# A two-layer decoder trunk on one core: new start addresses for the weight tiles and the transposed activations of the gate and up products, and four orders of their k steps

## The reference, cut to what matters

```python
def swiglu(x, w_gate, w_up, w_down):
    return (jax.nn.silu(x @ w_gate) * (x @ w_up)) @ w_down

for l in range(DEPTH):                       # DEPTH = 2
    x = x + 0.5 * swiglu(rms_norm(x, ffn1_norm[l]), ffn1_w_gate[l], ffn1_w_up[l], ffn1_w_down[l])
    h = rms_norm(x, mix_norm[l])
    proj = h @ w_in[l]                       # (256, 1024) @ (1024, 1184 + 2048)
    ...
    merged = jax.nn.sigmoid(g_a) * (o_a @ w_branch_a[l]) + jax.nn.sigmoid(g_b) * (o_b @ w_branch_b[l])
    x = x + merged @ w_out[l]
    x = x + 0.5 * swiglu(rms_norm(x, ffn2_norm[l]), ffn2_w_gate[l], ffn2_w_up[l], ffn2_w_down[l])
```

## Time and profile before

| what | value |
|---|---|
| median of 2 runs | 1039.3 us (1039.26 to 1039.33) |
| the profiled execution, its own time | 1040.34 us |
| its span, first to last instruction | 1038.5 us |
| granted TensorE clock | 1.000 |
| TensorE matmul busy (PE) | 1032.4 us, 99% |
| VectorE busy | 718.3 us, 69% |
| ScalarE busy | 586.1 us, 56% |

### The profile page before, as it was taken

The page is one execution under the profiler, slowest core; times in us unless marked ns, Lnnn a source line. Parts: engine busy times, 40 slices in busy tenths (PEclk is TensorE's granted clock), DMA queues, the critical chain, the costliest instruction groups (busy, mean ns, idle before and its releaser), DMA issues.

```text
span 1038.5 us, 15559 instructions
## 1 busy us (share of the span) xinstructions
PE 1032.4 (99%) x5648; PEld 891.7 (86%) x5648; DVE 718.3 (69%) x1132; ACT 586.1 (56%) x935; POOL 61.8 (6%) x71
## 2 busy tenths in 40 slices
PE   8999999999999999999999999999999999999998
PEld 7888888998888888888888888889988888888887
DVE  6766666668786876666687666666688868666665
ACT  6555454466963754554565455455678646454552
POOL 0052000121100000000000000001211000000000
PEclk9999999999999999999999999999999999999999
DMA  7665544455435455655445555534454346545541
GB/s 264 248 225 192 204 162 167 140 183 193 146 123 203 173 187 189 205 189 209 179 147 202 202 192 182 210 136 152 154 203 163 122 163 219 205 163 202 191 173 61
DMA packets 35269, 187.53 MB, mean 181 GB/s; under 512 B 4368, under 2 KB 4384, under 8 KB 20128
## 3 DMA queue, kind: packets, MB, share of 16 engines
q1 hardware_dynamic: 34992, 186.51, 51.0%
q0 software_dynamic: 240, 0.53, 0.2%
HBM read 185.98 MB, written 1.05 MB: 180 GB/s over the span
## 4 chain that ended last, share of the span: by engine, by line
PE 99%; DMA 1%; SPq 0%; DVE 0%; ACT 0%; issue 0%
PE ps L1369 96%; PE ps L1803 1%; PE ps L1393 1%; DMA w_raw<-in_w_ffn 1%; PE ps L1832 1%; PE ps L1868 0%; PE ps L1712 0%; PE ps L1704 0%; PE ps L1414 0%; DVE x_cols L999 0%; ACT w_hi L554 0%; SPq L318 0%; SPq L317 0%
## 5 line engine op out<-in xcount | busy, mean ns | idle before, releaser
L1369 PE MATMUL ps<-hT,w_hi 128*128 128x512 f32 x1408 | 341.3, 391 | 1.9 <-ACT w_hi L554 1.9
L1369 PEld LDWEIGHTS ps<-hT,w_hi 128*128 128x128 f32 x1408 | 258.9, 188 | 52.4 <-ACT w_hi L554 2.1
L884 DVE TENSOR_TENSOR w_lo<-w_raw,w_hi 128x2048 fp32r<-128x2048 f32 x82 | 188.0, 2293 | 87.7 <-ACT w_hi L549 87.7
L1369 PEld LDWEIGHTS ps<-hT,w_lo 128*128 128x128 f32 x1408 | 176.8, 188 | 7.5
L1369 PE MATMUL ps<-hT,w_lo 128*128 128x256 f32 x1408 | 178.3, 279 | 0.0
L1369 PE MATMUL ps<-w_hi,hT 128*128 128x512 f32 (+2 forms) x576 | 174.3, 377 | 0.0
L549 ACT ACTIVATE w_hi<-w_raw 128x2048 fp32r<-128x2048 f32 x85 | 162.0, 1906 | 13.9 <-PE ps L1369 13.2
L1369 PE MATMUL ps<-w_lo,aTh 128*128 128x512 f32 x352 | 137.2, 390 | 0.0
L1369 PE MATMUL ps<-w_hi,aTl 128*128 128x512 f32 x352 | 137.0, 389 | 0.0
L1369 PE MATMUL ps<-w_hi,aTh 128*128 128x512 f32 x352 | 136.8, 390 | 0.0
L578 ACT ACTIVATE S<-ps 128x256 f32<-128x256 f32 x88 | 33.7, 383 | 154.6 <-PE ps L1369 154.6
(11 more groups left out here) (168 smaller groups left out, 952.9 us busy)
## 6 DMA issues: line engine op xcount, KB each, us to landing
w_raw<-in_w_ffn SPq DMA_DIRECT2D x85, 1024.0 KB, 4.9
w_raw<-in_w_ffn SPq DMA_DIRECT2D x90, 512.0 KB, 5.7
w_raw<-in_w_gate SPq DMA_DIRECT2D x16, 1024.0 KB, 5.1
w_raw<-in_w_proj SPq DMA_DIRECT2D x16, 592.0 KB, 4.4
w_raw<-in_w_branch SPq DMA_DIRECT2D x8, 1024.0 KB, 4.8
w_raw<-in_w_out SPq DMA_DIRECT2D x8, 1024.0 KB, 4.8
w_raw<-in_w_uq SPq DMA_DIRECT2D x4, 384.0 KB, 3.0
w_raw<-in_w_ffn SPq DMA_DIRECT2D x4, 256.0 KB, 6.6
```

Of the source, the lines that this page charges most:

```text
L884: dve.tensor_tensor(wl_gu[b], raw_gu[b], wh_gu[b].bitcast(F32), ALU.subtract).then_inc(lo_gu.sem, 1)
L1369: return pe.matmul(dst, w, m, start=start, stop=stop, skip_group_check=True)
```

## The change

The four parts of the diff, in words:

- `hT` gets 12 unused columns behind each block of 512: blocks are `HT_STEP` = 524 columns = 2096 bytes apart (48 modulo 64).
- The gate and up chunks in `w_hi` and `w_lo` get 12 unused columns each: they are `K_STEP` = 140 columns = 560 bytes apart (48 modulo 64). Gate and up half tiles start at their own offsets in each slot, `HI_AT` and `LO_AT` (columns, for b = 0 and 1, gate and up). The low offset is always 8 columns (32 bytes) below the high one.
- In `gate_up` and `gate_up_low_first` the eight k steps run in one of four orders, by b and s (`K_ORDER`). All other functions keep the order 0 to 7.
- ScalarE's and VectorE's splitting instructions write (and VectorE reads back) the tile as 8 or 16 runs of 128 columns with the gaps between, instead of one run. Their number, sizes and order stay. The DMAs, and every wait and signal, stay.

```diff
-LO_SHIFT = 120
-LO_SLOT = GU_COLS + 128
+K_STEP, HT_STEP = P + 12, 2 * SEQ + 12
+HALF_STEP = 9 * P
+PART_SLOT = 2 * HALF_STEP + 64
+HI_AT, LO_AT = ((52, 40), (12, 16)), ((44, 32), (4, 8))
+K_ORDER = (((0, 1, 2, 3, 4, 5, 6, 7), (0, 2, 4, 6, 1, 3, 5, 7)),
+           ((7, 6, 5, 4, 3, 2, 1, 0), (0, 4, 1, 5, 2, 6, 3, 7)))
...
-        w_hi = sb("w_hi", [P, MIX_SLOTS * GU_COLS], F32R)
-        w_lo = sb("w_lo", [P, MIX_SLOTS * LO_SLOT], F32R)
+        w_hi = sb("w_hi", [P, 2 * PART_SLOT + GU_COLS], F32R)
+        w_lo = sb("w_lo", [P, 2 * PART_SLOT + GU_COLS], F32R)
...
+        def chunks(w, i, gate_at, up_at):
+
+            a, step = i * PART_SLOT + gate_at, HALF_STEP + up_at - gate_at
+            return w[:, a:a + 2 * step].rearrange("p (s n) -> p s n", s=2)[:, :, 0:KC * K_STEP]\
+                .rearrange("p s (k n) -> p s k n", k=KC)[:, :, :, 0:P]
+
+        def cols_of(w, c, n):
+
+            k = c // P % KC
+            part = w[:, c // (KC * P), k:k + n // P, :]
+            return part[:, 0, :] if n == P else part
...
+        wh_gu, wl_gu = ([chunks(w, i, *at) for i, at in enumerate(places)] for w, places in ((w_hi, HI_AT), (w_lo, LO_AT)))
...
-        hT = sb("hT", [P, KC, 2, SEQ], F32R)
+        hT_rows = sb("hT", [P, KC * HT_STEP + 32], F32R)
+        hT = hT_rows[:, 0:KC * HT_STEP].rearrange("p (k n) -> p k n", k=KC)[:, :, 0:2 * SEQ].rearrange("p k (s n) -> p k s n", s=2)
...
-                    act.activation(wh_gu[b], raw_gu[b], ACT.Copy).then_inc(hi_gu.sem, 1)
+                    act.activation(wh_gu[b], raw_gu[b].rearrange("p (s k n) -> p s k n", s=2, k=KC), ACT.Copy).then_inc(hi_gu.sem, 1)
...
-                    dve.tensor_tensor(wl_gu[b], raw_gu[b], wh_gu[b].bitcast(F32), ALU.subtract).then_inc(lo_gu.sem, 1)
+                    dve.tensor_tensor(wl_gu[b], raw_gu[b].rearrange("p (s k n) -> p s k n", s=2, k=KC), wh_gu[b].bitcast(F32), ALU.subtract).then_inc(lo_gu.sem, 1)
...
-                        for k in range(KC):
+                        for i, k in enumerate(K_ORDER[b][s]):
                             c = (s * KC + k) * P
-                            high(2 * b + s, wh_gu[b][:, c:c + P], k, k == 0)
+                            high(2 * b + s, cols_of(wh_gu[b], c, P), k, i == 0)
```

More of the change, by code:

```diff
@@ L117, in build @@
-        wl_d = [w_lo[:, 2 * LO_SLOT + i * DN_COLS:2 * LO_SLOT + (i + 1) * DN_COLS] for i in range(2)]
-        mix_raw, mix_hi = ([w[:, i * GU_COLS:(i + 1) * GU_COLS] for i in range(MIX_SLOTS)] for w in (w_raw, w_hi))
-        mix_lo = [w_lo[:, i * LO_SLOT:i * LO_SLOT + GU_COLS] for i in range(MIX_SLOTS)]
-        hT = sb("hT", [P, KC, 2, SEQ], F32R)
+        w_hi = sb("w_hi", [P, 2 * PART_SLOT + GU_COLS], F32R)
+        w_lo = sb("w_lo", [P, 2 * PART_SLOT + GU_COLS], F32R)
+        raw_gu = [w_raw[:, i * GU_COLS:(i + 1) * GU_COLS] for i in range(2)]
@@ new lines, in build @@
+        wh_gu, wl_gu = ([chunks(w, i, *at) for i, at in enumerate(places)] for w, places in ((w_hi, HI_AT), (w_lo, LO_AT)))
+        raw_d = [w_raw[:, 2 * GU_COLS + i * DN_COLS:2 * GU_COLS + (i + 1) * DN_COLS] for i in range(2)]
+        wh_d, wl_d = ([w[:, 2 * PART_SLOT + i * DN_COLS:2 * PART_SLOT + (i + 1) * DN_COLS] for i in range(2)]
+                      for w in (w_hi, w_lo))
+        mix_raw = [w_raw[:, i * GU_COLS:(i + 1) * GU_COLS] for i in range(MIX_SLOTS)]
+        mix_hi, mix_lo = ([w[:, i * PART_SLOT:i * PART_SLOT + GU_COLS] for i in range(MIX_SLOTS)] for w in (w_hi, w_lo))
@@ L561, in third_high @@
                     act.wait_ge(gu_used.sem, gu_used.at(0, 0))
-                    act.activation(wh_gu[0][:, part], third_raw[:, part], ACT.Copy)\
+                    act.activation(cols_of(wh_gu[0], part.start, KC * P), by_chunk(third_raw[:, part]), ACT.Copy)\
                        .then_inc((third_hi, hi_gu)[half].sem, 1)
@@ L715, in _ @@
                         act.wait_ge(landed.sem, 16)
-                        act.activation(wh_gu[1][:, part], raw_gu[1][:, part], ACT.Copy).then_inc(sig.sem, 1)
+                        act.activation(cols_of(wh_gu[1], part.start, KC * P), by_chunk(raw_gu[1][:, part]), ACT.Copy).then_inc(sig.sem, 1)
                     act.wait_ge(ss_clear.sem, 1)
@@ L1488, in gate_up_first @@
                             c = (s * KC + k) * P
[L1489 removed]
+                            high(s, cols_of(wh_gu[0], c, P), k, False)
                         if k == 0:
```

49 lines of the change are left out of this document (23 added, 26 removed).

## The result

The changed kernel takes 1049.96 us (1049.62 to 1050.31) against 1039.3: slower by 10.7 us, ratio 1.0101 with a 95% interval of 1.0084 to 1.0117. The time lies in the stated range, on the other side of no change from the forecast. The profiled execution took 1049.62 us with a span of 1047.8.

A forecast was written before the change was run, and what follows sets the result against it. It took TensorE, busy 99% of the span, as the bound, with only the gap between matmuls open to change. Terms of 0 and -0.7 us took 1040.3 to 1039.6, less 1.0 for the median: 1038.6 us, range 1020 to 1054.

The forecast's parts named there:

- The hint that I could not place: Gate and up: the gap behind a low is 10.2 ns against 13.3 to 13.6, from its distance or its shorter stream.
- Part 1: ScalarE's and VectorE's splitting copies: writing runs of 128 columns with gaps costs 0.
- Rival D: Splitting copies: gaps make them dear, delaying TensorE only if a tile takes 5.3 us longer; chance 0.04.
- Parts 2 and 3: Gate and up: steady blocks keep the weights-to-stream distance, so 0, between bounds of -33.5 and +13.2 us.
- The prediction's own sign: Gate and up: forecast wrong if the pace of high or low moves by more than 2 ns (2.8 us each).
- part 5: Mixing part, hT as weights at 48k: -0.7 us, crediting a quarter with 3.4 ns; bounds -11.7 and +4.1 us.
- rows 5 and 6: Profile rows of gate_up_first and of down behind low: an unsteady pace, up to 4.7 ns a matmul dearer.
- Rows 3: Profile rows of one steady loop turn: high 226.9 ns, low 116.9, down 226.7.
- rival C: Gate, up and mixing: new begins break the steady pace, 4.7 ns a matmul, +17.3 us to 1056.6; chance 0.18.
- Part 4: Thirteen blocks in plain k order, 416 matmuls, nearly all losing the distance: 0, bounds -5.0 and +2.0 us.
- Rival B: Gate and up: moving stream starts frees part of the gap, half giving -16.8 us, 1021.9 us; chance 0.28.
- A: Gate and up: the gap hangs on the kept distance or is fixed; the forecast, 1038.6 us; chance 0.50.

The follow-up runs named there:

- e9: Kernel before with aTh and aTl alone moved by 32 columns (128 bytes), so only the down weights lie elsewhere; 1046.3 us (1.0066).
- e11: Kernel before, but high gate and up weights too begin 32 bytes below a multiple of 256, like the low ones; 1048.5 us (1.0086).
- e12: Kernel before, but activation blocks (streams) 12 columns (48 bytes) later, gate and up weights unmoved; 1050.4 us (1.0102).
- e13: Kernel before, but high gate and up weights 12 columns (48 bytes) later, streams unmoved; 1048.3 us (1.0080).
- e15: Kernel before, but high weights of the four half tiles begin 4, 16, 32 and 48 columns past a multiple of 64; 1043.7 us (1.0037).
- e16: Kernel before, but all high gate and up weights begin 4 columns (16 bytes) past a multiple of 64 columns; 1042.8 us (1.0032).
- e6: Changed kernel with chunks 512 and blocks 2048 bytes apart again and the old weight places; the four k orders stay; 1039.8 us (1.0002).
- e19: Kernel before, but activations and gate and up weights all 16 columns (64 bytes) later, distance of weights and stream kept; 1044.1 us (1.0046).
- e18: Kernel before, but activations and gate and up weights all 32 columns (128 bytes) later, distance of weights and stream kept; 1042.1 us (1.0026).
- e7: Kernel before, but activations and gate and up weights all 12 columns (48 bytes) later, distance kept, plain order; 1048.9 us (1.0089).
- e8: Changed kernel with 16-column gaps, plain order, high weights at 48, low at 40: next high weights begin where the current stream began; 1050.7 us (1.0106).
- e10: Kernel before, but the low weights too begin at a multiple of 256 bytes instead of 32 bytes below one; 1043.5 us (1.0035).
- e2: Changed kernel with gaps of 16 columns instead of 12, all high tiles at offset 16 and low at 8; 1055.8 us (1.0158).
- run 120: Not a follow-up run: "run" is a verb here, and 120 ns is the first of the low matmuls' repeating times in the kernel before.

## Why the prediction was wrong

The runs together are described by this rule for the settled pace of 512 column streams, 226.7 ns. First, where no begin moves, the distance of weights and stream is 0 modulo 256 bytes (`e9`, `e11`, `e12`, `e13`, `e15`: 229 to 234 ns at 32, 48, 64 and 128 bytes to one side or the other; 16 bytes keep a settled pace and don't restore it, `e16`). Second, the common place is one that holds: 0, 64 and 128 bytes do, 48 doesn't (`e6`, `e19`, `e18`, `e7`). Third, the begins stay the same from one matmul to the next: where they move, the own and the next distance can't both be 0, and `e8`, whose next distance is 0 and whose own is 48 columns, doesn't settle. Where one of the three fails, TensorE stays in its unsettled pace, and hands it on to the next three to ten matmuls. Streams of 256 columns take 120.0 ns settled and 117 to 119 where the distance is off 0, so they gain by it.

The changed kernel's streams begin at 12k columns, off a multiple of 64 bytes at six of eight `high` matmuls. Its begins move at seven of eight, and its own distance is 52, 40, 12 or 16 columns at every one, by half tile. In the mixing part its weights lie 12k columns from their streams. That its addresses are the cause is shown: `e6` takes them back, keeps the order and the new slots, and has the old time. Which of these breaches holds it in the unsettled pace isn't separated, since every kernel with moving begins has an own distance off 0 as well, at nearly all of its `high` matmuls.

**What bounds the kernel** was right: TensorE's pace alone, a gap that doesn't grow with the stream. The gap of 13.3 ns is confirmed at a third length by `e10`. The hint that I could not place, 10.2 ns behind a `low`, is the distance of 8 columns and not the length by itself: 3.3 of the 3.4 ns.

**Part 1 (copies with gaps at 0)** was right, to the nanosecond. Rival D is out.

**Parts 2 and 3 hold the step that failed.** The prediction put it: "Between -33.5 and +13.2 I take 0, since the nearest row is the steady pace itself, at the same distance of weights and stream". The distance of the next weights from the current stream is indeed kept, and it isn't enough: `e8` keeps it too, at every step, and is as slow. What the term left out is the common place, which costs by itself (`e7`), and either the moving of the begins or the own distance, which was 0 for `high` before (`e8` has both, so the runs don't say which of the two). The prediction's own sign came: it calls itself wrong if the pace of `high` moves by more than 2 ns, and it moved by 4.0. The steady pace of before was no evidence for begins that move, because every stream of that kernel begins at one place. I also reckoned modulo 64 bytes, where `e9` shows that a distance of 128 bytes is as bad as any; the distances modulo 256 of the changed kernel's steady blocks happen to be the same, so this slip alone would not have changed parts 2 and 3; it bears on part 5, where 48k modulo 64 stood for 48k modulo 256.

The term was mis-sized thus: `high` +4.0 ns on the average (5.6 us) and `low` +1.2 (1.7 us), inside the bound of 4.7 that I had from rows 5 and 6. These rows were the right ones: 231.4 ns is the unsettled pace, a transient before and permanent now. Rows 3 held it too: `high` of the odd block takes 228.1 ns there, its first five being unsettled behind `low`, and the prediction read only the even block's 226.9 and said of rival C that the steady loop is free of it in `down`.

**Part 4** (plain order blocks at 0) fell the same way: outside the 35 turns `high` and `low` cost 0.8 us more, inside its upper bound of 2.0. **Part 5**, the mixing part at -0.7 us, came out at +1.9; the quarter that I had credited with the gap of `low` takes 229 to 237 ns in the first `gate` stage quoted above (k = 2 and 6), so it loses like the others. That a distance saves 3.4 ns for a stream of 256 columns could not be carried to 512 (`e11`: +6 ns).

**Rival C** is in substance what happened, at 0.18: new begins leave TensorE in the pace that it has behind a change of kind. Its price was too high, 17.3 us for 10.7. It took 4.7 ns for every matmul where `low` pays 1.2 only, and `proj`'s 384 columns next to nothing; and it had `down` at 226.7, where the first six pay in addition. **Rival B** is out: no begin brought the mean of a `high` half tile below 226.6 ns. That the measured time lies within the stated range is owed to C's share in it and says nothing for A.

By the Trainium skill (SBUF — State Buffer, "Specifications (TRN2)"), which has lines of 16 bytes as what costs, no kernel here should differ from the kernel before, since all begins are multiples of 16 bytes. The measurements disagree, by up to 16.7 us.

**What stays open.** Whether it is the change of begin that unsettles `e8` and the changed kernel, or that a chunk's own stream then lies elsewhere than the chunk itself (48 columns off in `e8`, where the next chunk's distance is 0); no run separates them. `e18` and `e19` show that a single change of begin with an own distance of 0 unsettles for one to ten matmuls, but the next distance is off 0 there; a kernel whose begins move at every step with an own distance of 0 was not tried. Why moved operands help short streams and hurt long ones: unsettled, 256 columns take about 118 ns and 512 about 232, which is less fixed cost and more per column, but that is a description, and no run reached the mechanism. Of common places off a multiple of 64 bytes only 48 was tried, so that 64 is the boundary is the simplest reading and not shown; 16 and 32 bytes were not tried.

## What to carry to other kernels

Where TensorE is the bound with float32r operands, let weights and streams of 512 column matmuls all begin at one and the same place modulo 256 bytes within the partition, at one of those that held here (0, 64 or 128 bytes, counted from the kernel's first tensor); put the weights of 256 column streams 32 bytes below it (116.7 ns against 120.0 in this kernel). Gaps, paddings and tensors of odd length ahead of an operand break this without a trace in the code: 32 columns more in one tensor cost 1056 untouched matmuls 5 ns each (`e2`), and 32 columns ahead of their own weights 6 ns (`e9`). And read such effects from the distance of starts in a steady loop, where a nanosecond shows; a pace seen there as a transient behind a change of kind can become permanent.

## What the runs showed of the hardware that I had not expected

- The settled pace of float32r matmuls at distance 0 is the columns and 13.3 ns: 120.0, 173.3 and 226.7 ns for 256, 384 and 512 columns.
- Instructions of one form at the same places have two paces, by what ran before them. With high weights 16 bytes past the stream's place, 512 columns take 226.7 ns behind settled matmuls and 233 behind unsettled ones, each for a whole block's `high`, on the mean of all 35 turns (`e16`).
- The pace repeats to the nanosecond: low matmuls with weights 32 bytes below the stream's place run 120, 113, 116, 117 ns over and over, and a turn of 88 matmuls takes 16460 ns with a standard deviation of 0.3 over 35 turns (kernel before).
- At 512 columns a distance of 128 bytes costs as much (232.9 ns, `e9`) as one of 48 (233, `e13`) or of -32 (233, `e11`), while a common shift by 128 or 64 bytes costs nothing once settled (226.7 ns, `e18` and `e19`).
